# A last expert's contribution split into high and low parts before it is placed, and one weight load moved in a queue

## What is computed

```python
a = jax.nn.silu(gate) * up * combine[:, :, None]          # combine: the two weights of a token
y = jnp.einsum("tef,efd->td", a, w_down)                  # hier_moe
...
moe = hier_moe(x, ...)
x = layer_norm(DEEPNORM_ALPHA * x + moe, ln2_g[i], ln2_b[i])
gate = jax.nn.sigmoid(jnp.einsum("bsd,de->bse", x, ple_w_gate[i]) + ple_b_gate[i])
x = x + gate * jnp.einsum("bsp,pd->bsd", p[i], ple_w_proj[i])
```

## Time and profile before

| | |
|---|---|
| median of three runs | 1264.56 us (1261.5 to 1265.8) |
| the profiled execution | 1262.75 us, its span 1261.2 us |
| PE busy | 1223.3 us, 97% of the span |
| DVE busy | 835.1 us, 66% |
| ACT busy | 558.8 us, 44% |
| POOL busy | 164.7 us, 13% |
| chain that ended last | PE 73%, DVE 12%, DMA 10%, ACT 3% |
| granted TensorE clock | 1.0 |

### The profile page before, as it was taken

One profiled execution on the slowest core, in us unless ns is written; L12 is line 12 of the kernel. 1 busy time (PEld: TensorE's weight loads), 2 busy tenths in 40 slices (PEclk: granted clock), 3 DMA queues, 4 the chain that ended last, 5 costly groups with the idle time before them and its releaser, 6 DMA issues.

```text
span 1261.2 us, 19733 instructions
## 1 busy us (share of the span) xinstructions
PE 1223.3 (97%) x7707; PEld 1110.1 (88%) x7707; DVE 835.1 (66%) x1122; ACT 558.8 (44%) x629; POOL 164.7 (13%) x193
## 2 busy tenths in 40 slices
PE   7999999999999999999999999999999999999998
PEld 6888899999999998888878699999998888877698
DVE  4654476464554745889889786445534889888793
ACT  4422332213121312478888563211221478878651
POOL 2200010010000002023231001000002022232100
PEclk9999999999999999999999999999999999999999
DMA  9444345242332422379999553221312369999512
GB/s 335 152 154 171 107 140 168 80 154 83 129 121 79 154 80 86 142 276 375 375 382 339 189 182 106 70 99 68 134 69 87 143 241 368 383 391 343 207 51 75
DMA packets 85616, 229.76 MB, mean 182 GB/s; under 512 B 9798, under 2 KB 42702, under 8 KB 73136
## 3 DMA queue, kind: packets, MB, share of 16 engines
q1 hardware_dynamic: 66880, 179.84, 39.5%
q0 software_dynamic: 18672, 49.04, 10.9%
HBM read 210.15 MB, written 35.46 MB: 195 GB/s over the span
## 4 chain that ended last, share of the span: by engine, by line
PE 73%; DVE 12%; DMA 10%; ACT 3%; issue 2%; POOL 1%; DVEq 0%; POOLq 0%; SPq 0%; ACTq 0%
PE ps L1776 14%; PE ps L1778 14%; PE ps L1777 14%; DMA w_raw<-in_moe_w_gate_up 7%; PE ps L1827 3%; PE ps L1829 3%; PE ps L1828 3%; DVE w_lo L1182 3%; PE ps L2133 2%; PE ps L2135 2%; PE ps L2134 2%; ACT w_hi L859 2%; PE ps L1887 2%; DVE x_tok L1605 2%; PE ps L2097 1%
## 5 line engine op out<-in xcount | busy, mean ns | idle before, releaser
L1182 DVE TENSOR_TENSOR w_lo<-w_raw,w_hi 128x2048 fp32r<-128x2048 f32 (+1 forms) x133 | 290.4, 2191 | 58.6 <-ACT w_hi L859 58.2
L1776 PE MATMUL ps<-x_hi,w_hi 128*128 128x288 f32 (+2 forms) x1024 | 305.0, 298 | 5.2 <-DVE w_lo L1182 3.7
L1778 PE MATMUL ps<-x_hi,w_lo 128*128 128x288 f32 (+2 forms) x1024 | 302.6, 296 | 0.0
L1777 PE MATMUL ps<-x_lo,w_hi 128*128 128x288 f32 (+2 forms) x1024 | 302.5, 295 | 0.0
L859 ACT ACTIVATE w_hi<-w_raw 128x2048 fp32r<-128x2048 f32 (+1 forms) x133 | 242.9, 1834 | 80.5 <-PE ps L1778 61.1
L1776 PEld LDWEIGHTS ps<-x_hi,w_hi 128*128 128x128 f32 x1024 | 193.3, 189 | 7.0 <-DVE w_lo L1182 4.4
L1777 PEld LDWEIGHTS ps<-x_lo,w_hi 128*128 128x128 f32 x1024 | 193.3, 189 | 0.1
L1778 PEld LDWEIGHTS ps<-x_hi,w_lo 128*128 128x128 f32 x1024 | 193.2, 189 | 0.0
L1776 PE MATMUL ps<-g_hi,w_hi 128*128 128x288 f32 x384 | 114.1, 297 | 1.3 <-DVE xT L1286 1.1
L1778 PE MATMUL ps<-g_hi,w_lo 128*128 128x288 f32 x384 | 113.4, 295 | 0.0
L1777 PE MATMUL ps<-g_lo,w_hi 128*128 128x288 f32 x384 | 113.2, 295 | 0.0
(11 more groups left out here) (308 smaller groups left out, 2120.2 us busy)
## 6 DMA issues: line engine op xcount, KB each, us to landing
w_raw<-in_moe_w_gate_up SPq DMA_DIRECT2D x34, 1024.0 KB, 10.7
w_raw<-in_moe_w_down SPq DMA_DIRECT2D x32, 1024.0 KB, 13.8
w_raw_more<-in_moe_w_gate_up SPq DMA_DIRECT2D x30, 1024.0 KB, 14.4
w_raw<-in_a_w_in SPq DMA_DIRECT2D x23, 1024.0 KB, 5.2
w_raw<-in_a_w_out SPq DMA_DIRECT2D x12, 1024.0 KB, 5.0
w_raw<-in_b_w_in SPq DMA_DIRECT2D x12, 1024.0 KB, 5.1
w_raw<-in_ple_w_gate SPq DMA_DIRECT2D x8, 1024.0 KB, 11.9
v_scratch<-v_stage POOLq DMA_DIRECT2D x6, 1024.0 KB, 4.6
```

The source lines that it names most:

```text
L1182: dve.tensor_tensor(unit_of(wlo, d), raw_unit(d), unit_of(whi, d).bitcast(f32), ALU.subtract).then_inc(split_done, 1)
L1776: pe.matmul(out, sh, mh, start=first, stop=False)
L1777: pe.matmul(out, sh, ml, start=False, stop=False)
L1778: ins = pe.matmul(out, sl, mh, start=False, stop=final)
```

## The change

For expert 15 the weight is taken out of the one-hot. ACT scales the evicted product by the slot's weight and rounds it (`last_y_hi`), DVE makes the rest (`last_y_lo`), and PE places both by a plain one-hot of ones in f32r, so that each half of a tile takes two f32r matmuls where one f32 matmul stood. Expert 14 keeps its weighted one-hot and plain f32. Expert 15's down product is done by column halves, and its first half is evicted while the second is computed. gate_load(1) goes behind rows_load(0), and ACT's `hi(U_G[l] + 1)` to just before `hi(U_G[l] + 2)`.

```diff
-                for j in range(2):
-                    gate_load(j)
+                gate_load(0)
...
                 rows_load(0)
+                gate_load(1)
                 sp.wait_ge(xtp, 2 * NE * (l + 1))
                 rows_load(1)
                 gate_load(2)
...
                     if s == NE - 1:
-                        for h, done in enumerate((y_half, y_cp)):
+                        for h, done in enumerate((y_first, y_cp)):
+                            if h == 0:
+                                act.wait_ge(y_half, l + 1)
+                                act.wait_ge(ohw_ok, l + 1)
+                            else:
+                                act.wait_ge(eu_used, EU * (l + 1))
                             act.activation(y_sb[:, 1, 512 * h:512 * h + 512], ps[:, down_bank(s) + h, :], ACT.Copy).then_inc(done, 1)
+                            act.wait_ge(done, l + 1 if h == 0 else NE * (l + 1))
+                            act.activation(ylh[:, 512 * h:512 * h + 512], y_sb[:, 1, 512 * h:512 * h + 512], ACT.Identity, scale=w_slot[:, 1:2]).then_inc(ylh_ok, 1)
                         return
...
-                hi(U_G[l] + 1)
                 y_out(NE - 1)
...
                 x_hi(0, PA, 4, KT)
+                hi(U_G[l] + 1)
                 hi(U_G[l] + 2)
...
-                for n in range(2):
-                    for i in range(2):
-                        ins = dve.tensor_scalar(ohw[:, n, i, :], iota[:, :], last_at[:, i, n:n + 1], w_slot[:, n:n + 1], ALU.is_equal, ALU.mult)
+                for i in range(2):
+                    dve.tensor_scalar(ohw[:, i, :], iota[:, :], last_at[:, i, 0:1], w_slot[:, 0:1], ALU.is_equal, ALU.mult)
+                    ins = dve.tensor_scalar(oh_last[:, i, :], iota[:, :], last_at[:, i, 1:2], None, ALU.is_equal)
...
+                def last_y_lo(h):
+                    dve.wait_ge(ylh_ok, 2 * l + h + 1)
+                    dve.scalar_tensor_tensor(out=yll[:, 512 * h:512 * h + 512], in0=y_sb[:, 1, 512 * h:512 * h + 512], scalar=w_slot[:, 1:2],
+                                             in1=ylh[:, 512 * h:512 * h + 512].bitcast(f32), op0=ALU.mult, op1=ALU.subtract).then_inc(yll_ok, 1)
...
                 add_rows(0, 0)
+                last_y_lo(0)
                 add_rows(0, 1)
+                last_y_lo(1)
                 add_rows(1, 0)
                 add_last(0)
...
-                    for a in range(2):
-                        for h in range(2):
...
+                    for a, h in ((0, 0), (0, 1), (1, 0), (1, 1)) if s < NE - 1 else ((0, 0), (1, 0), (0, 1), (1, 1)):
...
+                        if s == NE - 1 and a == 1 and h == 0:
+                            ins.then_inc(y_half, 1)
...
+                def late_rows(i):
+                    if i == 0:
+                        pe.wait_ge(ohw_ok, l + 1)
+                        pe.wait_ge(y_cp, NE * l + NE - 1)
+                    for h in range(2):
+                        pe.matmul(ps[:, LAST_BANK[i] + h, :], ohw[:, i, :], y_sb[:, 0, 512 * h:512 * h + 512], start=True, stop=False)
+
                 def last_rows(i):
...
+                    for h in range(2):
+                        out = ps[:, LAST_BANK[i] + h, :]
+                        if i == 0:
+                            pe.wait_ge(ylh_ok, 2 * l + h + 1)
+                        pe.matmul(out, oh_last[:, i, :], ylh[:, 512 * h:512 * h + 512], start=False, stop=False)
+                        if i == 0:
+                            pe.wait_ge(yll_ok, 2 * l + h + 1)
+                        ins = pe.matmul(out, oh_last[:, i, :], yll[:, 512 * h:512 * h + 512], start=False, stop=True)
                     ins.then_inc(ol_done, 1)
...
-                last_rows(0)
-                last_rows(1)
+                for i in range(2):
+                    late_rows(i)
+                    last_rows(i)
```

More of the change, by code:

```diff
@@ L294, in trunk @@
     aTf = xh("expert_actT_full", [P, F], f32, 32768)
-    ohw = at("last_onehot", [P, 2, 2, P], f32, S0 + 20992)
+    ohw = at("late_onehot_weighted", [P, 2, P], f32, S0 + 20992)
+    oh_last = at("last_onehot", [P, 2, P], f32r, S0 + 22016)
+    ylh = xh("last_y_hi", [P, D], f32r, 8192)
+    yll = xh("last_y_lo", [P, D], f32r, 28672)
     odn = xh("ovf_w_down", [P, 2, D], f32, 8192)
@@ L362, in trunk @@
         w_ok, side_st, wsl_ok, ohw_ok = sem("weights_ready"), sem("zeros_stored"), sem("slot_weights"), sem("last_onehot_ready")
-        y_half, ol_done = sem("last_y_half_copied"), sem("last_rows_summed")
+        y_half, ol_done = sem("last_y_half_product"), sem("last_rows_summed")
+        y_first = sem("last_y_half_copied")
+        ylh_ok, yll_ok = sem("last_y_hi_ready"), sem("last_y_lo_ready")
         n2_act = sem("x2_scaled_act")
@@ L997, in y_out @@
                 def y_out(s, it=0, step=0):
-                    act.wait_ge(eu_used, it * (3 * step) + (EU * l + dn_unit(s) + 1))
                     if l or s >= 2 or step:
@@ L1001, in y_out @@
                     if s == NE - 1:
-                        for h, done in enumerate((y_half, y_cp)):
+                        for h, done in enumerate((y_first, y_cp)):
[4 more added lines that the diff above has]
+                                act.wait_ge(eu_used, EU * (l + 1))
                             act.activation(y_sb[:, 1, 512 * h:512 * h + 512], ps[:, down_bank(s) + h, :], ACT.Copy).then_inc(done, 1)
+                            act.wait_ge(done, l + 1 if h == 0 else NE * (l + 1))
+                            act.activation(ylh[:, 512 * h:512 * h + 512], y_sb[:, 1, 512 * h:512 * h + 512], ACT.Identity, scale=w_slot[:, 1:2]).then_inc(ylh_ok, 1)
                         return
+                    act.wait_ge(eu_used, it * (3 * step) + (EU * l + dn_unit(s) + 1))
                     act.activation(y_sb[:, s % 2, :].rearrange("p (b t) -> p b t", b=2), ps[:, 4:6, :], ACT.Copy).then_inc(y_cp, 1)
@@ L2144, in down @@
                     pe.wait_ge(split_done, it * (3 * step) + (U_E[l] + e + 1))
-                    for a in range(2):
-                        for h in range(2):
[L2147 to L2152, removed]
+                    for a, h in ((0, 0), (0, 1), (1, 0), (1, 1)) if s < NE - 1 else ((0, 0), (1, 0), (0, 1), (1, 1)):
+                        out = ps[:, down_bank(s) + h, :]
+                        th, tl = aTh[:, P * a:P * a + P], aTl[:, P * a:P * a + P]
+                        wh, wl = [w4(w, e, 2 * a + h, 0, 512) for w in (whi, wlo)]
+                        pe.matmul(out, th, wh, start=(a == 0), stop=False)
+                        pe.matmul(out, th, wl, start=False, stop=False)
+                        ins = pe.matmul(out, tl, wh, start=False, stop=(a == 1))
+                        if s == NE - 1 and a == 1 and h == 0:
+                            ins.then_inc(y_half, 1)
                     ins.then_inc(eu_used, 1)
@@ L2181, in slot_weights @@
                     ins.then_inc(wsl_ok, 1)
-                def last_rows(i):
[L2184 to L2192, removed]
+                def late_rows(i):
[4 more added lines that the diff above has]
+                        pe.matmul(ps[:, LAST_BANK[i] + h, :], ohw[:, i, :], y_sb[:, 0, 512 * h:512 * h + 512], start=True, stop=False)
+                def last_rows(i):
+                    for h in range(2):
[6 more added lines that the diff above has]
+                        ins = pe.matmul(out, oh_last[:, i, :], yll[:, 512 * h:512 * h + 512], start=False, stop=True)
                     ins.then_inc(ol_done, 1)
```

## The result

The changed kernel took 1268.97 us, median of 9 runs (1267.45 to 1270.90). The kernel before, on the same chip, took 1264.20 (9 runs, 1261.50 to 1265.80). The ratio is 1.0041, 95% interval 1.0032 to 1.0049: slower by 0.41%, some 5 us. 1269.4 had been predicted. The total agrees; the parts agree less well, and most of this text is about that.

A forecast was written before the change was run, and what follows sets the result against it. Layer 2's chain was taken to run from scatter and row load through DVE, with PE and DVE within 0.26 us in layer 1. +2.5 (layer 2) and +2.3 (layer 1) make +4.8 on 1264.56: 1269.4 us, range 1264.5 to 1274.0.

The forecast's parts named there:

- Rival B: At DVE's wait before add_rows(1,0): tile 1's rows aren't held up, so not slower, about +1.0 us, 1265.6; chance 17%.
- T0: The moment SP issues rows_load(0), tile 0's rows; before, 696.2 in layer 1 and 1173.58 in layer 2.
- the 10.5 to 12: Sign in the profile after: the load of `x_gathered`, tile 1's rows, lands 10.5 to 12 us after T0.
- e: On SP's queue: delay of tile 1's rows' landing relative to T0 from gate_load(1) ahead; 3.2 us, bounds 2.65 to 4.3.
- g: At expert 13's scatter: how much earlier T0 comes without gate_load(1) beside it; 0.6 us in layer 1, 0.7 in layer 2.
- e - g: Net delay per layer from the load's move: 3.2 less 0.6 in layer 1, 3.2 less 0.7 (+2.5 us) in layer 2.
- layer 1's 0.26 of waiting for PE: Before add_last(0) in layer 1: DVE's 0.26 us wait for the placing matmuls, predicted to go.
- DVE's wait: Before add_rows(1,0): DVE idle 1.8 us for tile 1's rows, hiding the two last_y_lo of 0.65 each.
- ACT is ahead of DVE: At expert 15's scaled halves: ready at about 1179.2 and 1180.6, before DVE's 1179.5 and 1181.5, or a few tenths behind.
- Rival D: Split parts over 2.7 us late, so add_last(0) waits for PE; a microsecond at most; no separate chance given.
- Part 3: PE's placing matmuls: 5.3 us instead of 6.9, 1.6 less a layer but off the path; only layer 1's 0.26 gained.
- Rival C: PE's clock falls in a 3.5 us wait before tile 0's turn: +0.8 a layer, 1271.0, up to 1274; chance 12%.

The follow-up runs named there:

- e3: The changed kernel with gate_load(1) moved behind both tiles' row loads, ahead of gate_load(2): 1264.03 us, ratio 1.0003 to the kernel before.
- e1: The kernel before with only gate_load(1) between the two row loads and ACT's gate unit split moved; placing in plain f32: 1268.51 us, ratio 1.0035.
- e6: The changed kernel with gate_load(2) also put ahead of tile 1's row load, so two gate units ahead: 1279.16 us, ratio 1.0121 to the kernel before.
- e5: The changed kernel with 14 matmuls of ones instead of 6 ahead of tile 0's turn: 1265.89 us, ratio 1.0020 to the kernel before.
- e10: The changed kernel with 14 ones instead of 6 before tile 0's turn, plus 12 in the gate ahead of q = 6: 1267.86 us, ratio 1.0039.
- e2: The changed kernel with gate_load(1) back ahead of both tiles' row loads, leaving the split parts and column halves: 1264.91 us, ratio 1.0014.
- e7: The changed kernel with gate_load(1) behind both row loads and both last_y_lo behind both additions of tile 0's rows: 1262.56 us, ratio 0.9998.
- e4: The kernel before with gate_load(1) behind both tiles' row loads and ACT's gate unit split moved: 1263.07 us, ratio 0.9994.

## Why the prediction was right in its total, and its parts less so

**The order of the loads is the cause.** Predicted: tile 1's rows come late on SP's queue, behind one more megabyte. Shown: undone alone (e3), the loss goes; made alone (e1), it is there (1.0035 against 1.0041); doubled (e6), it grows to 1.2%. Rival B (the rows not held up) is refuted by e1's 3.38 and 2.91 us of DVE idle time. The landing in the changed kernel is 10.69 (695.84 to 706.53) and 10.55 (1175.38 to 1185.93) after T0, inside the 10.5 to 12 that were named.

**e was about right: 3.1 and 2.7, for 3.2.** Before, the rows landed 7.6 and 7.8 after T0. Both values lie in the bounds of 2.65 to 4.3, and so do those of e1, e5 and e10, which have the same order of loads: 2.8 to 4.0. The mean of these eight is 3.2.

**g was the mis-sized term: 1.27 and 1.73, not 0.6 and 0.7.** T0 moved from down - 2.73 to - 4.00, and from - 2.63 to - 4.36. Its bounds came from the quickest scatter in the rows, 4.5 us, and that one ran beside gate_load(2). I had noted this and still used 4.5 as the floor. Without the load, the scatter takes 4.0 (3.9 to 4.3 in the other traces); e1 and e2 show 3.97 and 5.72 without and with it. The prediction had said that it would be wrong if T0 moved by more than 1.5, and in layer 2 it did. So e - g, worked out as 2.6 and 2.5, was 1.8 and 1.0; with layer 1's 0.26 of waiting for PE gone and small differences in the start of DVE's steps, add_last(0) came 1.45 and 0.91 later. The queue thus accounts for 2.4 us and not for 4.8. That is one execution: by the same measure add_last(0) came 3.0 us later in e1, 3.6 in e5 and 4.0 in e10, both layers together. So the delay varies, but it was below the forecast in all four.

**DVE's wait was expected at 1.8 and was 0.77 and 0.27.** last_y_lo's printed duration is 0.75, but the next instruction starts 0.67 after it, so the 0.65 taken was near; ACT's scaling is printed at 0.72, its copy at 0.60. What counted is that with T0 earlier, DVE came to last_y_lo ahead of ACT, and waited 0.85 and 1.20 for it. "ACT is ahead of DVE" failed for the same reason as g: the rows moved forward, expert 15's product didn't. It cost nothing here, as the load was later still. The other runs bear it out: where T0 is as before (e2), DVE doesn't wait for ACT; where T0 and the load are both early (e3), it waits 0.70 and 1.01, and e7 has add_last(0) 0.7 earlier by avoiding most of that. Rival D had looked for late parts at PE; they were late at DVE.

**Part 3 and the rest of ACT.** add_last(0) starts without waiting for PE, as predicted. The gate unit's split moved behind x_hi held nothing up; ACT, timeline:

```profile
1198.42 3.70 ACT L864 ACTIVATE w_hi<-w_raw 128x2048 fp32r<-128x2048 f32 x2
1203.16 1.15 ACT L1075 ACTIVATE w_raw<-x_tok,mean_var 128x1024 f32<-128x1024 f32 x1 [1.03 <-DVE mean_var L1610]
```

Tile 2's squares still wait for DVE, 1.03 us in place of 2.84, with 1.9 of it used as worked out.

**Rival C makes up for most of the rest in the profiled execution.** It had a chance of 12% and a price of 0.8 a layer. The mechanism is shown for layer 1: turn 1.97 behind 2.31 us idle, DVE waiting 1.06 for it, 1.16 us at the gate. Layer 2 escaped, idle for 1.81. I had put PE's idle time at 3.5 in both, with add_last(0) at down + 9.1; it came at + 8.03 and + 7.53, and the idle time shrank by as much. What the rival did not name is that the clock also falls elsewhere, at gaps of 1.83 us in the gate's products that the kernel before has too: at 742 and 1220 in the changed kernel, at 1217 in e4, at about 740 in e1, e5 and e7 (which has one near 1217 too), at neither in the profiled execution before. It then costs time in some executions and none in others. Over the runs of all these kernels with a clock beside each time, a line fitted by least squares, with a level of its own for each kernel, gives 0.87 us (95%: +- 0.15) for each 0.001 of mean clock. The changed kernel's runs have a mean clock of 0.9958, those of the kernel before 0.9987 (74 runs, all from the batches of the experiments). That makes 2.5 us of the 5, an estimate, since a fit isn't a cause. e5 agrees: it halved the loss by filling the gap ahead of tile 0's turn and leaving the load alone. e10 doesn't: its clock was full and its loss whole. At full clock the same fit gives 1262.3 for the kernel before, and 1264.3 (e5), 1265.3 (the changed kernel), 1265.7 (e1) and 1266.7 (e10) for those with the late load. By this estimate the load costs 2.0 to 4.4 us by itself, and the clock has the rest.

So in the profiled execution the forecast's 4.8 was met by 2.4 us of the named mechanism and 2.6 (1.16 + 1.45) of a rival held unlikely, less 0.2 made good in between; a further 1.5 of the clock's, at 743, was hidden by a slow stretch of the execution that it is compared with. That the total agrees to half a microsecond is luck: two errors cancelled, g too small and the clock left out. Why the clock falls behind 1.83 us of idle time in one execution and not in the next is open; so are the two groups of times in e1 and e10.

## What to carry to other kernels

Where a load is taken up within 0.1 or 0.2 us of its landing, whatever is put ahead of it on its queue comes out at the end; put it behind all of the urgent loads, not between two of them. The floor of a transfer's time is not the quickest one in the trace unless that one ran alone. And when a wait moves, look what PE does meanwhile: a delay of 1.5 us elsewhere cost 1.2 more through the clock, and in the two traces with eight more matmuls of ones in the gap (e5 and e10), the turn was at full speed.

## What the runs showed that I had not expected

- The indirect scatter of expert 13 took 5.4 and 6.0 us beside a load of 1 MB, issued 8.7 us ahead of it in layer 2, and 4.0 without it: 1.4 and 2.0 us less.
- The second megabyte ahead of a load cost more than the first: tile 1's rows landed 7.2 and 7.4 after their issue with none, 9.7 and 9.6 with one (up to 10.8 in other executions), 14.2 and 13.0 with two.
- The granted clock fell behind idle times of 1.83 to 2.31 us of PE, but not each time: of the eighteen waits of the gate of 1.83 to 1.85 in the nine traces that have them, eight were followed by a fall, and 2.16 passed in e1. In e2 it fell behind two shorter ones close together, 0.74 (at 1115) and 0.90 (at 1117). So in these traces the length of a single gap doesn't tell whether the clock falls.
- At equal mean clock, executions of the same kernel lie in two groups 3.5 us apart when tile 1's rows are late (e10: 1265.1 to 1265.2, and 1267.9 to 1269.3).
